# Where the scan's gate products stand: two parts moved from the inverse's last levels to the end of each scan step

## The chip, the cores and the metric

One core of one Trainium2 chip runs the whole program. The metric is the device time of one execution in microseconds. Two kernels are compared by their runs on the same chip.

## The reference, cut to what matters

The model is one inference step through two layers, over 128 context tokens and 512 latent tokens (five blocks of 128). In each layer a mixing part has four branches. The outputs of the branches are weighted by gates and summed:

```
proj  = einsum('blnw,nwd->blnd', branches, w_branch)
gates = sigmoid(h @ w_gate + b_gate)
out   = einsum('blnd,blnd->bld', gates, proj) @ w_out
```

The gates need only `h`, so they can be computed at any time before the projection. One branch is a scan over time in two directions and with four heads, whose state is 64 x 64 per head:

```
sa = einsum('bhvk,bhk->bhv', S, -kk_t)
S  = S * w_t + sa * (kk_t * a_t) + v_t * k_t
y  = einsum('bhvk,bhk->bhv', S, r_t)
```

The rest of a layer (local attention, a convolution, a spatial gate, the mixture of experts) is not touched here.

## The kernel before

**The scan in steps.** The kernel does the scan in chunks of 128 tokens. `STEPS` lists five steps of a layer, numbered 0 to 4 here; a step does one block of the forward and one of the backward direction, so eight (direction, head) pairs side by side. Within a step the recurrence becomes a triangular system. Its inverse `TT` is built on TensorE by doubling: first the 32 x 32 diagonal blocks (four levels, `INNER` = 4, the loop from L1129), then level `INNER` joins them to 64 x 64 (from L1151), and level `INNER + 1` joins those to 128 x 128 (from L1173). Each level has two sets of small products with a copy between them: TensorE makes X (semaphore `x_mm`), ScalarE copies X out of PSUM (L1575, at the last level L1578, semaphore `xm_done`), TensorE multiplies by the other factor (`y_mm`, at the last level `yt_mm`), and VectorE puts the result into the inverse (L1989 and L1991 for the inner levels; L2001, L2006 and L2011 at level `INNER`; L2022 at level `INNER + 1`, semaphore `t_done`). GpSimd copies the four diagonal blocks into `TT` (L819, `tt_done`), which the last level's second products wait for.

**The step's end.** With the inverse there, TensorE makes U from the old state and the values (`u_mm`); then the first two terms of the outputs y (they need nothing new); then, when ScalarE has copied U (L1581, `u_done`), the inverse times U (`sa_mm`). ScalarE negates that into `sa` (L1584, `sa_done`), and TensorE makes the last term of y and the new state (`step_mm`). VectorE adds both up (L2036 to L2043, `step_done`) and goes straight on to the next step's first operations (from L1915), which ScalarE's square root and sigmoids (L1398, L1555, L1556) and TensorE's decay sums wait for.

**The gate products as filler.** The gate product of a layer is cut into 64 units of 320 tokens by 128 columns; each unit has two parts of four k-tiles, and `PARTS` lists these 128 parts in order. Each part is twelve fp32r products of 128 x 128 by 128 x 320. `behind(lo, hi)` issues parts `lo` to `hi` on TensorE. Part 0 of a unit issues eight small products for the modulation ahead of them (`micro_rows`, 128 x 64 rows in the trace), and in odd units two more products (`micro_columns`); its own waits are for the bank (the sigmoid two units back), for the split weights, and for the loaded modulation weights. `behind_out` is ScalarE's side: after part 1 of a unit it copies the modulation row (L1466), takes the sigmoid (L1472) and, in even units, rounds the next 128 x 1024 weight chunk (L1448). `rests_behind` is VectorE's side: the rest of that chunk (L1747), also after part 1 of even units. SyncE's queue loads the modulation weights two units ahead (L669), loads the weight chunks (L663) and stores the gates to HBM (L690), each behind the semaphore of the unit's products or sigmoid.

**Where the parts stand.** The order is written out by hand: each engine's program names the same ranges of parts at the same places. A step owns 13 parts (`STEP_PARTS`). Its first parts fill the waits of the step's preparation; from `part + LEVELS_FROM` on, each of the six levels has one range, `level_parts(part, lev)`, issued between a level's X products and its second products:

```python
    lo = part + LEVELS_FROM + lev
    return lo, closed(part + STEP_PARTS) if lev == LEVELS - 2 else lo + 1
```

So level `INNER` has one part and level `INNER + 1` the rest of the step: `closed` rounds up to a whole unit. In steps 0, 2 and 4 the two levels have parts 0 and 1 of one unit. In steps 1 and 3 level `INNER` has part 1 of a unit, and level `INNER + 1` both parts of the next. That is 12 parts of a layer at these two levels, 24 in all. The rest of a weight chunk (L1747) falls among them in step 1 and step 2 (at level `INNER + 1`) and in step 3 (at level `INNER`).

Of the kernel before, what the change touches and what calls it, by code (L numbers as in the profile page):

```python
# [157 lines left out]
INNER = LEVELS - 3  # L158
# [82 lines left out]
def build(nc, a):  # L241
    ctx = ExitStack()
    with ctx:
# [182 lines left out]
        def bank(b, n=512):  # L426
            return ps[:, b * 512:b * 512 + n]
# [438 lines left out]
        def _(pe):  # L866
# [93 lines left out]
            with pe.Fori(0, DEPTH) as layer:  # L960
# [121 lines left out]
                for s, blocks in enumerate(STEPS):  # L1082
# [72 lines left out]
                            early, late = halves_of(g // 4, h)  # L1155
                            ins = mm(bank(4)[late, g * QB:(g + 1) * QB], gb[early, g, 0, late], Tc[early, g])
                    ins.then_inc(x_mm, 1)
                    behind(*level_parts(part, INNER))
                    pe.wait_ge(xm_done, now.next("xm_done"))
                    pe.wait_ge(ttc_done, now.next("ttc_done", 2))  # L1160
                    pe.sem_inc(waits_settled, 1)
# [15 lines left out]
                        early, late = rows64 if g < 4 else rows64[::-1]  # L1177
                        ins = mm(bank(0)[late, g * HD:(g + 1) * HD], gb[early, g, 0, late], T64[early, g % 4])
                    ins.then_inc(x_mm, 1)
                    behind(*level_parts(part, INNER + 1))  # L1180
                    pe.wait_ge(xm_done, now.next("xm_done"))
                    pe.wait_ge(ttc_done, now.next("ttc_done", 2))
                    pe.wait_ge(tt_done, now.next("tt_done"))
# [20 lines left out]
                    for g in range(8):  # L1204
                        ins = mm(by_row_half(2, g), gk[:, g, 0, :], v_of(g), False, g >= 6)
                    ins.then_inc(u_mm, 1)
                    for g in range(8):
                        of = rows64[g % 2]
                        mm(by_row_half(0, g), ar[of, g // 2, 1, :], S0[of, g // 2], g < 2, False)
# [3 lines left out]
                    for g in range(8):  # L1213
                        ins = mm(bank(2)[:, g * HD:(g + 1) * HD], TT[:, g], ub[:, g])
                    ins.then_inc(sa_mm, 1)
                    pe.wait_ge(sa_done, now.next("sa_done"))
                    for g in range(8):
                        mm(by_row_half(0, g), gb[:, g, 1, :], sa[:, g], False, g >= 6)
# [157 lines left out]
        def _(act):  # L1376
# [111 lines left out]
            with act.Fori(0, DEPTH) as layer:  # L1488
# [62 lines left out]
                for s, blocks in enumerate(STEPS):  # L1551
                    part = SCAN_AT + s * STEP_PARTS
                    root(kss)
                    act.wait_ge(wa_pre, now.next("wa_pre"))
                    A(sw, sw, ACT.Sigmoid)  # L1555
                    A(aa, aa, ACT.Sigmoid).then_inc(wa_done, 1)  # L1556
                    behind_out(closed(part), part + WA_PARTS)
                    act.wait_ge(decay_mm, now.next("decay_mm"))
                    A(rt.rearrange("p d c -> p (d c)"), bank(2), ACT.Exp)
                    A(bt.rearrange("p d c -> p (d c)"), bank(2), ACT.Exp, scale=-1.0)  # L1560
                    A(at_.rearrange("p d c -> p (d c)"), bank(3), ACT.Exp)
                    A(gm.rearrange("p g e -> p (g e)"), bank(4, 8), ACT.Exp).then_inc(exp_done, 1)
                    behind_out(part + WA_PARTS, closed(part + 5))
                    act.wait_ge(tildeT_mm, now.next("tildeT_mm"))
                    nc.scalar.copy(ar[:, :, 0, :], bank(0).rearrange("p (g t) -> p g t", g=4))
                    nc.scalar.copy(bT, bank(2).rearrange("p (g t) -> p g t", g=4)).then_inc(tildeT_act, 1)
                    behind_out(closed(part + 5), closed(part + 6))
                    act.wait_ge(n_mm, now.next("n_mm"))
                    nc.scalar.copy(nb.rearrange("p (g r) t -> p r g t", r=2),
                                   ps[:, 2048:3072].rearrange("p (r c) -> p r c", r=2)[:, :, 0:4 * QB].rearrange("p r (g t) -> p r g t", g=4)  # L1570
                                   ).then_inc(nc_done, 1)
                    behind_out(closed(part + 6), part + LEVELS_FROM)
                    for lev in range(INNER + 1):
                        act.wait_ge(x_mm, now.next("x_mm"))
                        nc.scalar.copy(Xq.rearrange("p g t -> p (g t)"), bank(4, 8 * QB)).then_inc(xm_done, 1)  # L1575
                        behind_out(*level_parts(part, lev))
                    act.wait_ge(x_mm, now.next("x_mm"))
                    nc.scalar.copy(Xc.rearrange("p g t -> p (g t)"), bank(0)).then_inc(xm_done, 1)  # L1578
                    behind_out(*level_parts(part, INNER + 1))
                    act.wait_ge(u_mm, now.next("u_mm"))  # L1580
                    nc.scalar.copy(ub.rearrange("p (g r) v -> p r g v", r=2),  # L1581
                                   ps[:, 1024:2048].rearrange("p (r g v) -> p r g v", r=2, g=8)[:, :, 0:4]).then_inc(u_done, 1)
                    act.wait_ge(sa_mm, now.next("sa_mm"))
                    nc.scalar.mul(sa.rearrange("p g v -> p (g v)"), bank(2), -1.0).then_inc(sa_done, 1)  # L1584
                root(gs2)
                behind_out(closed(NORM_AT), len(PARTS))
                micro_column_out(CHUNKS - 1, 6)
# [108 lines left out]
        def _(dve):  # L1696
# [97 lines left out]
            with dve.Fori(0, DEPTH) as layer:  # L1794
# [111 lines left out]
                for s, blocks in enumerate(STEPS):  # L1906
# [105 lines left out]
                                                  bank(2, 8 * QB)[early, 4 * d * QB:4 * (d + 1) * QB].rearrange("p (g t) -> p g t", g=4),  # L2012
                                                  -1.0, None, ALU.mult)
                    ins.then_inc(ttc_done, 2)
                    rests_behind(*level_parts(part, INNER))
                    dve.wait_ge(tc_done, now.next("tc_done"))
                    dve.wait_ge(ttc_done, now.next("ttc_done", 2))
                    blocks64 = (slice(0, 64), slice(64, P))
# [3 lines left out]
                        ins = V.tensor_scalar(TT[early, 4 * d:4 * d + 4, late], bank(3).rearrange("p (g t) -> p g t", g=8)[early, 4 * d:4 * d + 4],  # L2022
                                              -1.0, None, ALU.mult)
                    ins.then_inc(t_done, 1)
                    rests_behind(*level_parts(part, INNER + 1))

                    dve.wait_ge(step_mm, now.next("step_mm"))
                    for d, blk in enumerate(blocks):
# [23 lines left out]
                    else:  # L2052
                        ins.then_inc(step_done, 1)
                    dve.wait_ge(step_done, now.next("step_done"))

                rests_behind(closed(NORM_AT), len(PARTS))
                y20 = y.rearrange("p b (h c) -> p (b h) c", h=4)
# [368 lines left out]
```

## Time and profile before

| | |
|---|---|
| Median of 3 runs | 2786.13 us (2786.0 to 2787.79) |
| The profiled execution's own time | 2792.74 us |
| Its span, first to last instruction | 2791.2 us |
| Mean granted clock of TensorE in it | 0.885 |
| TensorE products, busy | 2248.3 us (81%) |
| VectorE, busy | 1388.4 us (50%) |
| ScalarE, busy | 995.0 us (36%) |
| GpSimd, busy | 228.9 us (8%) |

The scan of layer 0 lies from about 461 to 829 us of the span, that of layer 1 from about 1830 to 2205 us. Busy shares over the span mix stages with different limits; in the scan the engines work in a chain, and what counts is which of them the next one waits for. The granted clock of TensorE is a share of full speed: 1.00 is 2.4 GHz, 0.50 is 1.2 GHz.

### The profile page before, as it was taken

Reading aid. Unit: us, or ns where it says so; the run is one execution under the profiler, and the core shown is the slowest. Engines: PE = TensorE matmul, PEld = TensorE weight load, DVE = VectorE, ACT = ScalarE, POOL = GpSimd, SP = SyncE. Lnnn points to the kernel's source line nnn. Section 1 sums busy time; section 2 is a strip of 40 time slices with the busy share of each in tenths; the row PEclk is TensorE's granted clock in tenths of the full one; section 3 lists DMA queues with packets and bytes.
Section 4 is the critical chain, followed back from the end, with each engine's and each line's share of the span. In section 5 each row is a group of like instructions: output and inputs, shape, how many; then the busy total and the mean of one; then the engine's idle time right before and its main releaser. Section 6 shows DMA issues by size and latency. Waiting matters only on the chain.

```text
span 2791.2 us, 50199 instructions
## 1 busy us (share of the span) xinstructions
PE 2248.3 (81%) x20372; PEld 1899.2 (68%) x20372; DVE 1388.4 (50%) x1773; ACT 995.0 (36%) x1448; POOL 228.9 (8%) x251
## 2 busy tenths in 40 slices
PE   4998698898888975989459896888888799588980
PEld 2787688787774764777248785877878658467760
DVE  2225834434346544888242275344343373458873
ACT  3113234222220133777241323432232102257771
POOL 0002111101110001000100031111011000200001
PEclk9998899989898977999769998999898799589995
DMA  7114322323226307999722242233233252279986
GB/s 316 61 61 129 99 84 91 104 85 100 92 88 233 141 36 271 396 392 397 282 85 91 86 136 73 74 112 104 88 105 93 104 210 91 113 294 396 398 333 248
DMA packets 102282, 466.89 MB, mean 167 GB/s; under 512 B 12160, under 2 KB 28800, under 8 KB 75008
## 3 DMA queue, kind: packets, MB, share of 16 engines
q1 hardware_dynamic: 81792, 352.36, 34.8%
q0 software_dynamic: 10320, 75.91, 7.3%
q10 hardware_dynamic: 9936, 35.35, 3.1%
q8 instruction: 166, 2.72, 0.4%
q14 instruction: 68, 0.56, 0.1%
HBM read 389.64 MB, written 94.90 MB: 174 GB/s over the span
## 4 chain that ended last, share of the span: by engine, by line
PE 55%; issue 19%; DVE 9%; DMA 6%; ACT 6%; POOL 4%; SPq 0%; DVEq 0%; ACTq 0%; POOLq 0%
PE ps L870 53%; ACT we_hi L1629 3%; PE ps L873 3%; DVE we_lo L2223 2%; POOL wg_lo L763 2%; DMA x_kept<-x 1%; DMA arena<-in_experts 1%; DMA arena<-expert_out,slots 1%; POOL expert_rows L844 1%; DMA expert_out<-rows 1%; DVE arena L2253 1%; DMA rests_last<-hz_lo 1%; DMA arena<-expert_rows 0%; DVE arena L1989 0%; POOL arena L811 0%
## 5 line engine op out<-in xcount | busy, mean ns | idle before, releaser
L2223 DVE TENSOR_TENSOR we_lo<-arena,we_hi 128x2048 fp32r<-128x2048 f32 x150 | 339.3, 2289 | 92.5 <-ACT we_hi L1629 92.5
L870 PE MATMUL ps<-hz_hi,wg_hi 128*128 128x320 f32 x1024 | 349.6, 341 | 24.6 <-DMA rests_last<-hz_lo 19.0
L870 PE MATMUL ps<-arena 32*32 32x32 f32 (+5 forms) x7408 | 295.6, 225 | 53.7 <-DVE arena L1989 14.2
L870 PE MATMUL ps<-hz_hi,wg_lo 128*128 128x320 f32 x1024 | 330.9, 323 | 0.0
L870 PEld LDWEIGHTS ps<-arena 32*32 32x32 f32 (+4 forms) x7408 | 206.8, 120 | 146.7 <-issue 143.7
L1629 ACT CAST we_hi<-arena 128x2048 fp32r<-128x2048 f32 x150 | 282.9, 1912 | 3.2 <-DMA arena<-in_experts 2.9
L873 PE MATMUL ps<-fix,arena 128*128 128x128 f32 x836 | 133.8, 305 | 164.3 <-DMA arena<-expert_rows 65.9
L870 PE MATMUL ps<-rests,wg_hi 128*128 128x320 f32 x768 | 249.8, 325 | 0.0
L873 PEld LDWEIGHTS ps<-fix,arena 128*128 128x128 f32 x836 | 107.8, 156 | 189.1 <-DMA arena<-expert_rows 66.1
L870 PEld LDWEIGHTS ps<-hz_hi,wg_hi 128*128 128x128 f32 x1024 | 204.7, 200 | 39.3 <-issue 22.0
L870 PEld LDWEIGHTS ps<-hz_hi,wg_lo 128*128 128x128 f32 x1024 | 205.9, 201 | 0.0
L870 PE MATMUL ps<-wz_hi,hz_hi 128*128 128x512 f32 (+1 forms) x480 | 181.6, 378 | 17.3 <-DVE x L1723 17.3
L870 PE MATMUL ps<-wz_hi,hz_lo 128*128 128x512 f32 (+1 forms) x480 | 180.7, 376 | 0.0
L870 PE MATMUL ps<-w_lo,hz_hi 128*128 128x512 f32 (+1 forms) x480 | 180.5, 376 | 0.0
L870 PE MATMUL ps<-we_hi,te_hi 128*128 128x512 f32 x400 | 159.4, 399 | 8.8 <-DVE te_lo L2228 8.8
L870 PE MATMUL ps<-we_hi,te_lo 128*128 128x512 f32 x400 | 158.9, 397 | 0.0
L870 PE MATMUL ps<-we_lo,te_hi 128*128 128x512 f32 x400 | 158.7, 397 | 0.0
L870 PEld LDWEIGHTS ps<-rests,wg_hi 128*128 128x128 f32 x768 | 156.3, 204 | 0.0
L763 POOL TENSOR_TENSOR wg_lo<-ring,wg_hi 128x1024 fp32r<-128x1024 f32 x32 | 77.3, 2417 | 769.5 <-ACT wg_hi L1448 769.5
L1840 DVE SCALAR_TENSOR_TENSOR x<-x,cols 128x655 f32<-128x655 f32 x120 | 132.3, 1144 | 2.1
L1739 DVE TENSOR_TENSOR w_lo<-ring,wz_hi 128x2048 fp32r<-128x2048 f32 x24 | 55.0, 2293 | 142.1 <-ACT wz_hi L1423 142.1
L1466 ACT COPY combT<-ps 128x64 f32<-128x64 f32 x128 | 26.8, 210 | 261.3 <-PE ps L870 261.3
(309 smaller groups left out, 4040.0 us busy)
## 6 DMA issues: line engine op xcount, KB each, us to landing
arena<-in_experts SPq DMA_DIRECT2D x150, 1024.0 KB, 8.9
ring<-in_stream SPq DMA_DIRECT2D x26, 2048.0 KB, 8.4
ring<-in_gate_stream SPq DMA_DIRECT2D x64, 512.0 KB, 3.9
arena<-in_mod_stream SPq DMA_DIRECT2D x128, 256.0 KB, 3.1
expert_rows<-in_stream POOLq DMA_DIRECT2D x50, 512.0 KB, 5.6
arena<-expert_rows SPq DMA_DIRECT2D x50, 512.0 KB, 7.1
expert_out<-rows ACTq DMA_DIRECT2D x50, 512.0 KB, 8.2
gates<-arena SPq DMA_DIRECT2D x128, 160.0 KB, 2.6
```

The costliest lines, as they stand in the source:

```text
L763: nc.gpsimd.tensor_tensor(wg_lo[q % 2], wg[q % 2], wg_hi[q % 2].bitcast(F32), ALU.subtract).then_inc(pool_split, 1)
L844: pool.indirect_dma_start(rows_dram, to, hm[:, b, :], None).then_inc(rows_sent, 16)
L870: return nc.tensor.matmul(out, lhsT, rhs, start=start, stop=stop)
L873: return nc.tensor.transpose(out, in_, ident)
L1466: nc.scalar.copy(micro_row[q % 2][:, at:at + MICRO], bank(bk)[:, HALF:HALF + MICRO]).then_inc(mod_rows, 1)
L1629: nc.scalar.copy(we_hi[n % HIS], raw[n % RAW]).then_inc(piece_hi, 1)
L1739: V.tensor_tensor(half_in(w_lo, v), half_in(ring, v), wz_hi[v % 2].bitcast(F32), ALU.subtract).then_inc(wlo_done, 2)
L1840: ins = V.scalar_tensor_tensor(cacc[f], src, cw[:, f, t:t + 1], cacc[f], ALU.mult, ALU.add)
L2223: V.tensor_tensor(we_lo[n % RAW], raw[n % RAW], we_hi[n % HIS].bitcast(F32), ALU.subtract).then_inc(piece_split, 1)
L2253: V.tensor_tensor(te_hid[i % 2], te_silu[i % 2], ps[:, (i % 2) * 512 + FF:(i % 2) * 512 + 2 * FF], ALU.mult).then_inc(hid_done, 1)
```

## The change

In each scan step the parts of level `INNER` are issued behind the U products, ahead of the first two terms of y. Those of level `INNER + 1` are issued behind the product of the inverse and U, ahead of the wait for `sa_done`. ScalarE's side moves with them: the first range behind its copy of U, the second behind its negation into `sa`. VectorE's side moves too: the rest of a chunk at level `INNER` behind the last operation on the inverse (L2022), that of level `INNER + 1` behind the state's update, ahead of the next step's first operation. No part is added or left out, and the order of the parts is the same.

```diff
--- before.py
+++ after.py
@@ -1155,7 +1155,6 @@
                             early, late = halves_of(g // 4, h)
                             ins = mm(bank(4)[late, g * QB:(g + 1) * QB], gb[early, g, 0, late], Tc[early, g])
                     ins.then_inc(x_mm, 1)
-                    behind(*level_parts(part, INNER))
                     pe.wait_ge(xm_done, now.next("xm_done"))
                     pe.wait_ge(ttc_done, now.next("ttc_done", 2))
                     pe.sem_inc(waits_settled, 1)
@@ -1177,7 +1176,6 @@
                         early, late = rows64 if g < 4 else rows64[::-1]
                         ins = mm(bank(0)[late, g * HD:(g + 1) * HD], gb[early, g, 0, late], T64[early, g % 4])
                     ins.then_inc(x_mm, 1)
-                    behind(*level_parts(part, INNER + 1))
                     pe.wait_ge(xm_done, now.next("xm_done"))
                     pe.wait_ge(ttc_done, now.next("ttc_done", 2))
                     pe.wait_ge(tt_done, now.next("tt_done"))
@@ -1204,6 +1202,7 @@
                     for g in range(8):
                         ins = mm(by_row_half(2, g), gk[:, g, 0, :], v_of(g), False, g >= 6)
                     ins.then_inc(u_mm, 1)
+                    behind(*level_parts(part, INNER))
                     for g in range(8):
                         of = rows64[g % 2]
                         mm(by_row_half(0, g), ar[of, g // 2, 1, :], S0[of, g // 2], g < 2, False)
@@ -1213,6 +1212,7 @@
                     for g in range(8):
                         ins = mm(bank(2)[:, g * HD:(g + 1) * HD], TT[:, g], ub[:, g])
                     ins.then_inc(sa_mm, 1)
+                    behind(*level_parts(part, INNER + 1))
                     pe.wait_ge(sa_done, now.next("sa_done"))
                     for g in range(8):
                         mm(by_row_half(0, g), gb[:, g, 1, :], sa[:, g], False, g >= 6)
@@ -1573,15 +1573,17 @@
                     for lev in range(INNER + 1):
                         act.wait_ge(x_mm, now.next("x_mm"))
                         nc.scalar.copy(Xq.rearrange("p g t -> p (g t)"), bank(4, 8 * QB)).then_inc(xm_done, 1)
-                        behind_out(*level_parts(part, lev))
+                        if lev < INNER:
+                            behind_out(*level_parts(part, lev))
                     act.wait_ge(x_mm, now.next("x_mm"))
                     nc.scalar.copy(Xc.rearrange("p g t -> p (g t)"), bank(0)).then_inc(xm_done, 1)
-                    behind_out(*level_parts(part, INNER + 1))
                     act.wait_ge(u_mm, now.next("u_mm"))
                     nc.scalar.copy(ub.rearrange("p (g r) v -> p r g v", r=2),
                                    ps[:, 1024:2048].rearrange("p (r g v) -> p r g v", r=2, g=8)[:, :, 0:4]).then_inc(u_done, 1)
+                    behind_out(*level_parts(part, INNER))
                     act.wait_ge(sa_mm, now.next("sa_mm"))
                     nc.scalar.mul(sa.rearrange("p g v -> p (g v)"), bank(2), -1.0).then_inc(sa_done, 1)
+                    behind_out(*level_parts(part, INNER + 1))
                 root(gs2)
                 behind_out(closed(NORM_AT), len(PARTS))
                 micro_column_out(CHUNKS - 1, 6)
@@ -2012,7 +2014,6 @@
                                                   bank(2, 8 * QB)[early, 4 * d * QB:4 * (d + 1) * QB].rearrange("p (g t) -> p g t", g=4),
                                                   -1.0, None, ALU.mult)
                     ins.then_inc(ttc_done, 2)
-                    rests_behind(*level_parts(part, INNER))
                     dve.wait_ge(tc_done, now.next("tc_done"))
                     dve.wait_ge(ttc_done, now.next("ttc_done", 2))
                     blocks64 = (slice(0, 64), slice(64, P))
@@ -2022,7 +2023,7 @@
                         ins = V.tensor_scalar(TT[early, 4 * d:4 * d + 4, late], bank(3).rearrange("p (g t) -> p g t", g=8)[early, 4 * d:4 * d + 4],
                                               -1.0, None, ALU.mult)
                     ins.then_inc(t_done, 1)
-                    rests_behind(*level_parts(part, INNER + 1))
+                    rests_behind(*level_parts(part, INNER))
 
                     dve.wait_ge(step_mm, now.next("step_mm"))
                     for d, blk in enumerate(blocks):
@@ -2052,6 +2053,7 @@
                     else:
                         ins.then_inc(step_done, 1)
                     dve.wait_ge(step_done, now.next("step_done"))
+                    rests_behind(*level_parts(part, INNER + 1))
 
                 rests_behind(closed(NORM_AT), len(PARTS))
                 y20 = y.rearrange("p b (h c) -> p (b h) c", h=4)
```

## Rows read from the trace of the kernel before

**Rows 1.** The page's first line.

```profile
span 2791.2 us, 50199 instructions
```

**Rows 2.** Step ends, L2022 to L2043, by windows: length, TensorE busy, granted clock, DMA.

```profile
514.28:529.46 15.18, 13.53 (x142) 0.89 0.17 46
587.81:609.75 21.94, 20.29 (x136) 0.56 0.03 9
...
814.38:828.67 14.29, 10.87 (x128) 1.00 0.04 14
...
sum 186.18, PE 166.15; mean PE 16.61
```

**Rows 3.** The timeline of step 2 in layer 0, its last two levels and end.

```profile
657.20 0.48 PE L870 MATMUL ps<-arena,x 32*32 32x32 f32 x32 [0.61 <-DVE arena L1989]
657.61 0.43 PE L870 MATMUL ps<-arena,silu_c_padded 128*32 128x64 f32 x16
657.63 1.47 DVE L2001 COPY arena<-arena 32x128 f32<-32x128 f32 x4
657.77 1.70 POOL L819 COPY arena<-arena 32x256 f32<-32x256 f32 x4 [21.88 <-DVE arena L1991]
...
659.92 0.71 PE L870 MATMUL ps<-arena 32*32 32x32 f32 x48
660.67 0.59 DVE L2006 TENSOR_SCALAR arena<-ps 32x128 f32<-32x128 f32 x2 [1.57 <-PE ps L870]
...
661.41 0.68 PE L870 MATMUL ps<-arena,x 64*64 64x64 f32 x16 [0.78 <-DVE arena L2006]
662.02 0.41 PE L870 MATMUL ps<-hz_hi,wg_hi 128*128 128x320 f32 x1
662.13 0.59 ACT L1578 COPY arena<-ps 128x512 f32<-128x512 f32 x1 [4.02 <-PE ps L870]
...
663.97 0.68 PE L870 MATMUL ps<-arena 64*64 64x64 f32 x16
664.80 0.86 DVE L2022 TENSOR_SCALAR arena<-ps 64x256 f32<-64x256 f32 x2 [2.32 <-PE ps L870]
665.76 1.11 PE L870 MATMUL ps<-scan_state_scaled,arena 64*128 64x64 f32 x16 [1.11 <-issue]
...
668.84 0.58 ACT L1581 COPY x<-ps 128x512 f32<-128x512 f32 x1 [3.15 <-PE ps L870]
...
673.59 0.60 ACT L1584 ACTIVATE x<-ps 128x512 f32<-128x512 f32 x1 [4.17 <-PE ps L870]
...
674.24 0.99 PE L870 MATMUL ps<-x 128*128 128x64 f32 x7 [0.69 <-ACT x L1584]
```

**Rows 4.** VectorE groups by line: busy, mean ns | idle before them, releaser.

```profile
L2006 DVE TENSOR_SCALAR arena<-ps 32x128 f32<-32x128 f32 x20 | 5.7, 286 | 9.9 <-PE ps L870 9.8
L2022 DVE TENSOR_SCALAR arena<-ps 64x256 f32<-64x256 f32 x20 | 8.4, 422 | 30.0 <-PE ps L870 29.8
```

**Rows 5.** Windows with TensorE's clock: step 2's inner levels; y in steps 2, 3.

```profile
641.45:645.20 3.75, 1.18 (x66) 1.00 0.16 52
645.20:648.05 2.85, 2.18 (x82) 0.51 0.00 0
648.05:651.55 3.50, 3.50 (x16) 0.50 0.27 80
652.03:655.60 3.57, 2.87 (x123) 1.00 0.02 5
668.73:671.60 2.87, 2.87 (x33) 1.00 0.00 0
742.78:748.15 5.37, 5.37 (x34) 0.50 0.01 3
```

**Rows 6.** VectorE's rest of a weight chunk, in the groups by line.

```profile
L1747 DVE TENSOR_TENSOR wg_lo<-ring,wg_hi 128x1024 fp32r<-128x1024 f32 x32 | 39.4, 1230 | 22.1 <-ACT wg_hi L1448 21.0 <-issue 0.3
```

**Rows 7.** The timeline of TensorE at the decay sums of step 3.

```profile
685.08 1.13 PE L870 MATMUL ps<-arena,scan_sums 128*128 128x256 f32 x4 [0.78 <-ACT arena L1556]
```

## The prediction

> **What bounds the kernel now.** I start from the profiled execution: a span of 2791.2 us [rows 1], 2792.74 us by its own time, 6.6 us above the median of the runs shown. The change touches only the ten scan steps (five in each of two layers), so I read the scan. I cut out the ten step ends, from VectorE's last operation on the inverse (L2022) to the new state (L2043), with TensorE's granted clock beside each [rows 2]. The reader should see that the same work takes 14.29 us at clock 1.00 (one step end of the ten), 15.2 to 15.4 us at 0.89 (four) and 21.9 to 22.6 us at 0.55 to 0.57 (five). TensorE is busy nearly all that time, so the slow ends don't wait more: they run at 1.2 instead of 2.4 GHz. All ten last 186.18 us; at full clock they would last 142.9, so the clock costs 43.3 us there.
>
> Then I read one step in order of time [rows 3]. TensorE, ScalarE and VectorE hand on to each other, and a gate part between them costs path time where it is longer than the wait that it fills.
>
> **Level INNER.** In step 2 the X products start at 657.20; modulation rows and the part fill TensorE from 657.61 until the second products start at 659.92, so 2.31 us stand there. Twelve gate products alone take 1.95 us (662.02 to 663.97 at the next level), so the modulation rows take 0.36. Without them the second products wait for ScalarE's copy of X. Its double-sized sibling L1578 takes 0.59 us, so they end by about 659.06. But L2006, which they feed, stands behind four copies on VectorE (L2001) that end at 659.10; these become the limit. L2006 then starts right behind L2001, and what is saved is exactly VectorE's idle time before L2006: 9.9 us over ten steps [rows 4] (1.57 in step 2). Behind the U products the same part covers nothing: the next work, the first two y terms, needs no one, and they hide ScalarE's copy of U (0.58 us) already. So it costs its whole length there. Per layer that is five parts of 1.95, three sets of modulation rows of 0.36 and two pairs of column products. I have no row for a pair: between 0 and 0.36 us, taken as 0.30, nearer the modulation rows because it too loads 128-column weights. This makes 11.4 us a layer and 22.9 for both. Net: 22.9 - 9.9 = **+13.0 us**.
>
> **Level INNER + 1.** Step 2: products start at 661.41, the part at 662.02, the second products at 663.97. ScalarE's copy ends at 662.72; GpSimd's diagonal blocks are there at 659.47. So these products could start at about 662.75, which leaves 1.1 of the 2.32 us of VectorE's idle time before L2022. Over ten steps that idle time is 30.0 us [rows 4], and in step 3 of both layers a chunk rest of 1.23 us lies in the same gap and hides 2.5 more. Saved: 30.0 + 2.5 - 11.0 = 21.5 us. At the new place the parts fill the wait for `sa`, 0.69 us in each step [rows 3], and the rest is on the path. Per layer there are seven parts, two sets of modulation rows and one column pair, 14.7 us; for both layers 29.3. Net: 29.3 - 6.9 - 21.5 = **+0.9 us**.
>
> **The queues the moved work passes.** ScalarE's sigmoid, row copy and chunk rounding now stand between U and `sa`. They start when the part ends, and the y terms (2.87 us [rows 5]) and the product with the inverse lie ahead of `sa`: nothing. Those of the last range run beside the state's products. SyncE's loads and gate stores go out later by the same few us, as do their users: nothing, and if a buffer ran late a part would wait for it. GpSimd's copies, done at 659.47 in step 2, have 1.7 us to spare: the second products would start at about 661.2 there, L2006 being 1.57 us earlier (663.97 - 1.22 - 1.57). VectorE's chunk rests are different. At level INNER (step 3) the rest runs beside U. At level INNER + 1 (steps 1 and 2) it now stands at the head of the next step's chain, whose end TensorE awaits: in step 3 the decay sums start after 0.78 us of idleness, released by ScalarE's sigmoid [rows 7], which follows VectorE. I take the whole 1.23 us [rows 6], four times: **+4.9 us**; the lower bound is 0, if the chain had slack.
>
> **The clock.** This is the large term, and it has two signs. Full clock at all step ends would give back the 43.3 us. But the level work loses its fill. See what such a stretch does in step 2's inner levels [rows 5]: from 641.45 to 648.05 TensorE ran small products with waits between, the clock was 1.00 until 645.20 and 0.50 from there. The part that followed ran at 0.50, 3.50 us instead of 1.95, and at 652.03 the clock was back. After the change every step has a stretch of that kind: in step 2 from the last inner part (its end is the edge of the window that ends at 655.60 [rows 5]) to U (665.76 - 1.57 - 1.22 = 662.97), 7.4 us against the 6.6 us of the example. Before, the gap without a part ahead of U was 663.97 to 665.76, and even behind that the clock was down for most of five of the ten ends. So I expect the clock to fall ahead of U in all ten steps. Dense products of the end don't bring it back: the y terms take 5.37 us at 0.50 in step 3 against 2.87 in step 2, busy throughout [rows 5]. The moved part of level INNER does, as in the example. The loss per step: U has as many products as the y terms, 2.5 us; the 64 x 64 products about 0.3 (from 0 to their doubling, 1.2; taken near the bottom because waits dominate there); and the part and the start of y until the clock returns, from 0 to 1.75 (the 1.55 of a whole part and some 0.2 of y). The example, where it returned only behind the part, says the upper half: 1.2. Together 4.0 us a step (2.5 to 5.4), **+40 us** for ten. From there on the end holds full clock: y ran through at 1.00 in step 2, and the gap ahead of the new state that now stops TensorE is filled. So **-43.3 us** on the other side. The median, 6.6 us below the profiled execution, may have had one slow end less (8.3 us); then it is -35.
>
> **Sum.** 13.0 + 0.9 + 4.9 + 40 - 43.3 = +15.5 us. On the median of 2786.13 us that is 2801.6; in a profiled execution about 2808.
>
> **Rivals.**
>
> First, **the clock follows how busy TensorE is**, so it is back as soon as U runs without a gap, and holds to the end of the step; the 40 us vanish. The Trainium skill, "TensorE: Matmul & The Clock Gate", section "What's actually happening", says that the gate is set by how busy the array has been recently; by that rule this rival would be the outcome. For it: the new ends have no gap behind the wait for `t_done`, as U, the parts, y and the state stand one behind the other. Against it: y at 0.50 was busy 5.37 of 5.37 us [rows 5], so busy time alone doesn't raise the clock here. It decides at one place, U of each step: if U takes 3 us there, and not 5.4, the time is 2786.1 + 18.8 - 43.3 = 2761.6, **faster**. Chance 0.15.
>
> Second, **the clock returns early and the chunk rests are hidden**: the loss is 3.0 us a step and VectorE's chain has slack. 13.9 + 30 - 43.3 = +0.6, or +5.5 with the rests: 2787 to 2791.6, no change that can be told. The place is the start of the moved part; it decides if less than 0.5 us of it runs at 0.50. Chance 0.14.
>
> Third, **one part isn't enough to raise the clock**, and each end stays at 0.50 as five do now. Per step, U 2.5, the part 1.55, y 2.5, the product with the inverse 1.7 (1.99 us from 671.60, the edge of a window [rows 5], to 673.59 [rows 3], by y's ratio of 1.87), the last parts about 2 and the state about 2.5 (by the same ratio): 12.7 us, ten times 127 - 43.3 + 18.8 = +102, 2889. Against it is the example, where one part sufficed. Chance 0.03.
>
> That the change doesn't do what it says has no room: no semaphore is added, and each moved range waits for things older than before.
>
> **How the numbers follow.** The forecast, slower, has 0.68. A measurement of this kernel can tell about 0.2%, 5.6 us, from no change. Slower by more: the forecast and the third rival, 0.71; within: 0.14; faster: the first, 0.15. The forecast's own bounds: with 3.2 us lost per step and the rests hidden, +2.6; with 5.0 and one slow end fewer before, +33.8. The range of 2783 to 2820 takes both in and leaves out the first and third rivals, 0.18.
>
> **What would show it.** Right: in each of ten steps the clock goes to 0.50 between the last inner part and U, U takes 5 to 5.5 us, the clock is 1.00 from y to the state, and the stretch from L2022 to L2043 lasts about 23 us in steps 0, 2 and 4 and 24 in steps 1 and 3, with the parts in it. L2006 follows L2001 without a gap, idle time before L2022 is 1.1 us, and the decay sums of steps 2 and 3 start 1.2 us later behind L2043. Wrong: U at 3 us (first rival), a moved part that is at full clock from its start (second), or a state product at 0.50 (third).

## The result, and the profile after

| | before | after |
|---|---|---|
| Median, same chip | 2786.74 us (2786.0 to 2787.79, 4 runs) | 2834.4 us (2814.75 to 2837.61, 4 runs) |
| Ratio, 95% interval | | 1.0156 (1.0109 to 1.0203) |
| Profiled execution, its span | 2792.74 us, 2791.2 us | 2837.61 us, 2836.0 us |
| Mean granted clock in it | 0.885 | 0.868 |

The change makes the kernel slower by 47.7 us. The forecast was slower, by 15.5 us, with a range that ended 34 us above the kernel before: the direction held, the size did not.

First the ten step ends, from VectorE's first operation on the last level's result (L2023 now) to the new state (L2044 now). They are the windows of [rows 2] in the changed kernel, with length, TensorE's busy time, granted clock, DMA share and GB/s:

```profile
513.45:536.20 22.75, 21.79 (x198) 0.74 0.15 43
594.95:618.00 23.05, 22.10 (x207) 0.80 0.17 50
673.34:694.62 21.28, 20.32 (x195) 0.79 0.07 22
...
sum 226.16, PE 213.03; mean PE 21.30
```

Before, the ends were of two kinds, five near 15 and five near 22 us. Now all ten take 21.2 to 23.9 us at 0.74 to 0.82. The timeline of step 2, beside [rows 3], says where in an end the clock is low:

```profile
667.70 1.47 DVE L2003 COPY arena<-arena 32x128 f32<-32x128 f32 x4
...
669.37 0.59 DVE L2008 TENSOR_SCALAR arena<-ps 32x128 f32<-32x128 f32 x2 [0.20 <-PE ps L870]
...
670.10 1.12 PE L870 MATMUL ps<-arena,x 64*64 64x64 f32 x16 [0.78 <-DVE arena L2008]
671.26 0.59 ACT L1579 COPY arena<-ps 128x512 f32<-128x512 f32 x1 [3.05 <-PE ps L870]
...
672.08 1.12 PE L870 MATMUL ps<-arena 64*64 64x64 f32 x16 [0.86 <-ACT arena L1579]
673.34 0.86 DVE L2023 TENSOR_SCALAR arena<-ps 64x256 f32<-64x256 f32 x2 [2.16 <-PE ps L870]
674.30 1.97 PE L870 MATMUL ps<-scan_state_scaled,arena 64*128 64x64 f32 x16 [1.10 <-issue]
676.20 3.67 PE L870 MATMUL ps<-arena,x 128*128 128x64 f32 x16
...
683.27 1.11 PE L870 MATMUL ps<-scan_state_scaled,arena 64*128 64x64 f32 x16
```

U is the pair of rows from 674.30. Its first sixteen products take 1.97 us, and the same sixteen of y behind the moved part take 1.11 at 683.27. The 64 x 64 products take 1.12 instead of the 0.68 of [rows 3]. L2008 follows L2003 by 0.20 us where 1.57 lay between them. Windows of the same step show the clock itself:

```profile
666.00:674.30 8.30, 4.28 (x177) 0.67 0.51 148
674.30:680.40 6.10, 6.10 (x49) 0.50 0.01 3
680.40:682.41 2.01, 2.01 (x11) 0.50 0.30 89
682.41:694.62 12.21, 12.21 (x141) 1.00 0.07 22
```

U and the modulation rows of the moved part are busy throughout and stay at 0.50; so do the first seven of the part's own twelve products; from 682.41 to the end of the step the clock is 1.00. This is the picture that the prediction drew, and all ten steps show it. VectorE's groups, beside [rows 4]:

```profile
L2023 DVE TENSOR_SCALAR arena<-ps 64x256 f32<-64x256 f32 x20 | 8.4, 422 | 20.5 <-PE ps L870 20.4
L2008 DVE TENSOR_SCALAR arena<-ps 32x128 f32<-32x128 f32 x20 | 5.7, 286 | 1.5 <-PE ps L870 1.3
```

The idle time before L2008 is gone, as forecast (9.9 us, now 1.5). That before L2023 fell from 30.0 to 20.5 and not to 11.

To see the rest I cut the scan into seven stretches and summed each over its steps, in the two profiled executions: A from the new state to the next second sigmoid (L1556; eight gaps), B to VectorE's copy at L1970 (L1968 before), C to L2008 (L2006), D to L2023 (L2022), E to ScalarE's copy of U, F to `sa`, G to the new state.

| us | A | B | C | D | E to G | ten steps | all else |
|---|---|---|---|---|---|---|---|
| before | 35.6 | 127.6 | 338.4 | 50.4 | 186.2 | 738.2 | 2053.0 |
| after | 40.8 | 145.6 | 330.0 | 38.4 | 226.2 | 781.0 | 2055.0 |
| difference | +5.2 | +18.1 | -8.5 | -12.0 | +40.0 | +42.8 | +2.1 |
| forecast | +4.9 | 0 | -9.9 | -18.5 | +39.0 | +15.5 | 0 |

The forecast of E to G is 22.9 + 29.3 - 6.9 for the parts, 25 for U and 12 for the part at low clock, less 43.3. Stretch B, which the prediction did not look at, holds most of what is missing. Two lines of its windows, step 1 of layer 0 and the sum, in the changed kernel:

```profile
541.01:560.42 19.41, 17.59 (x114) 0.74 0.25 80
...
sum 145.64, PE 137.93; mean PE 13.79
```

and in the kernel before:

```profile
534.28:549.00 14.72, 12.95 (x114) 1.00 0.33 105
...
sum 127.57, PE 120.44; mean PE 12.04
```

It is the same work, 114 products, at a lower clock. Why it fell there is seen at the decay sums with which B begins. Here is the timeline at them, before, in steps 1 and 2:

```profile
534.94 1.99 PE L870 MATMUL ps<-arena,scan_sums 128*128 128x256 f32 x8 [1.42 <-ACT arena L1556]
...
614.74 1.99 PE L870 MATMUL ps<-arena,scan_sums 128*128 128x256 f32 x8 [0.17 <-ACT arena L1556]
```

and after:

```profile
541.68 2.99 PE L870 MATMUL ps<-arena,scan_sums 128*128 128x256 f32 x8 [2.24 <-ACT arena L1556]
...
624.29 3.67 PE L870 MATMUL ps<-arena,scan_sums 128*128 128x256 f32 x8 [4.49 <-ACT arena L1556]
```

TensorE now stands idle for 2.24 and 4.49 us ahead of them, and the clock falls while they run. Over the eight step starts that follow a step of the same layer, this idle time was 10.8 us and is 25.7; at 1.00 in all eight before, the clock falls in five of them now.

### The profile page after: what moved, and what is told of

It reads as the page before. It is cut to its first block, busy times and chain, and to the rows that moved or that the text cites. A ratio compares the mean times of both kernels' runs of the same rounds, so it can differ in the third digit from the quotient of the medians.

```text
span 2836.0 us, 50199 instructions
## 1 busy us (share of the span) xinstructions
PE 2259.6 (80%) x20372; PEld 1912.2 (67%) x20372; DVE 1389.1 (49%) x1773; ACT 995.8 (35%) x1448; POOL 228.7 (8%) x251
## 4 chain that ended last, share of the span: by engine, by line
PE 55%; issue 19%; DVE 9%; DMA 7%; ACT 6%; POOL 4%; SPq 0%; DVEq 0%; ACTq 0%; POOLq 0%
PE ps L870 52%; ACT we_hi L1631 3%; PE ps L873 3%; DMA arena<-in_experts 2%; POOL wg_lo L763 2%; DVE we_lo L2225 2%; DMA x_kept<-x 1%; DMA arena<-expert_out,slots 1%; POOL expert_rows L844 1%; DMA expert_out<-rows 1%; DMA rests_last<-hz_lo 1%; DVE arena L2255 1%; DMA arena<-expert_rows 0%; DVE arena L1991 0%; POOL arena L811 0%
## 5 line engine op out<-in xcount | busy, mean ns | idle before, releaser
L870 PE MATMUL ps<-hz_hi,wg_hi 128*128 128x320 f32 x1024 | 357.4, 349 | 24.7 <-DMA rests_last<-hz_lo 19.0
L870 PE MATMUL ps<-arena 32*32 32x32 f32 (+5 forms) x7408 | 303.2, 228 | 70.9 <-DVE arena L1991 14.3
L870 PE MATMUL ps<-hz_hi,wg_lo 128*128 128x320 f32 x1024 | 337.3, 329 | 0.0
L870 PEld LDWEIGHTS ps<-arena 32*32 32x32 f32 (+4 forms) x7408 | 213.4, 123 | 162.3 <-issue 158.6
L870 PEld LDWEIGHTS ps<-hz_hi,wg_hi 128*128 128x128 f32 x1024 | 211.0, 206 | 39.1 <-issue 22.5
L870 PEld LDWEIGHTS ps<-hz_hi,wg_lo 128*128 128x128 f32 x1024 | 212.5, 207 | 0.0
```

Source lines behind the costliest of these rows:

```text
L870: return nc.tensor.matmul(out, lhsT, rhs, start=start, stop=stop)
```

## The experiments

Each run has its own kernel before on the same chip. The stages outside the scan, which no kernel here changes, took 2034 to 2057 us between the profiled executions, so where 20 us matter I compare the ten steps in the traces, and give the ratio of the runs beside it. The traces are one execution of each kernel. In the expectations below the second to fifth experiments are rests_early, after_warm, before_warm and after_warm_start, and "the third of these" is ahead_of_u.

| kernel | ratio, 95% interval | ten steps | A | B | C | D | E | F | G |
|---|---|---|---|---|---|---|---|---|---|
| before | | 738.2 | 35.6 | 127.6 | 338.4 | 50.4 | 46.2 | 68.4 | 71.6 |
| after | 1.0156 (1.0109 to 1.0203) | 781.0 | 40.8 | 145.6 | 330.0 | 38.4 | 65.7 | 86.6 | 73.8 |
| after_again | 1.0137 (1.0076 to 1.0199) | 780.7 | 40.8 | 146.8 | 327.8 | 39.4 | 65.7 | 86.3 | 73.9 |
| inner_back | 1.0224 (1.0184 to 1.0264) | 801.5 | 40.8 | 142.3 | 337.7 | 33.3 | 64.6 | 89.2 | 93.6 |
| before_warm | 0.9904 (0.9872 to 0.9936) | 704.2 | 35.6 | 135.2 | 339.8 | 50.4 | 40.3 | 47.5 | 55.4 |
| after_warm | 0.9987 (0.9961 to 1.0012) | 739.1 | 40.8 | 148.7 | 332.1 | 33.4 | 40.9 | 69.4 | 73.9 |
| rests_only | 1.0058 (1.0031 to 1.0086) | 757.3 | 40.8 | 134.7 | 340.3 | 50.4 | 44.4 | 72.5 | 74.1 |
| rests_early | 1.0145 (1.0093 to 1.0197) | 781.7 | 35.6 | 135.8 | 328.6 | 39.0 | 65.7 | 98.2 | 78.7 |
| start_warm_only | 1.0082 (1.0053 to 1.0112) | 774.8 | 40.8 | 135.9 | 333.1 | 39.8 | 65.7 | 85.7 | 73.9 |
| after_warm_start | 0.9861 (0.9795 to 0.9928) | 713.3 | 40.8 | 139.0 | 316.4 | 32.7 | 41.3 | 69.4 | 73.9 |
| before_warm_start | 0.9889 (0.9823 to 0.9954) | 707.2 | 35.6 | 133.9 | 340.3 | 54.2 | 40.3 | 47.5 | 55.4 |
| after_warm_rests | 0.9876 (0.9829 to 0.9923) | 702.3 | 35.6 | 134.4 | 314.0 | 33.2 | 40.9 | 69.3 | 74.7 |
| ahead_of_u | 0.9908 (0.9874 to 0.9942) | 718.2 | 35.6 | 136.3 | 337.2 | 33.0 | 64.2 | 47.5 | 64.4 |
| ahead_of_u_warm | 0.9892 (0.9864 to 0.9921) | 714.9 | 35.6 | 134.0 | 341.0 | 32.8 | 68.5 | 47.5 | 55.4 |

**after_again**, the changed kernel a second time.

> The changed kernel, nothing altered, for a second profiled execution. Which of the terms recur? Theory: the fall ahead of U is set by where the parts stand: in all ten steps 6.57 us from the first result of the last level to ScalarE's copy of U, the state's products at 1.00 in nearly all; and the falls in the step starts are a consequence of the change too, so the stretch from the second sigmoid to the copy at L1970 sums to 140 to 150 again (127.6 in the kernel before), the ten steps to 775 to 787. Rival: the falls in the starts were this one execution's; then that stretch sums to 127 to 134 and the ten steps to 760 to 770. Stages outside the scan, which the change does not touch, may differ by 20 us either way.

E, F and B came out at 65.7, 86.3 and 146.8, within 1.2 us of the first execution: both the fall ahead of U and the slower step starts came back, though not in the same starts.

**inner_back**: level `INNER` undone (all three engines), the last level's parts left behind the inverse's product. TensorE's side of the edit, against the changed kernel:

```diff
                     ins.then_inc(x_mm, 1)
+                    behind(*level_parts(part, INNER))
...
                     ins.then_inc(u_mm, 1)
-                    behind(*level_parts(part, INNER))
```

> The change with level INNER's range put back to its old place on all three engines; only the last level's parts stand behind the product with the inverse. Theory (the clock falls where the parts are missing ahead of U, and only parts bring it back): the stretch without a part now runs from the last level's X products to the end of the product with the inverse, so the clock is at 0.50 over U, the y terms and that product in most steps (about 6.7 us each), and at 1.00 in the state's products. In the sum +0.9 for the last level, +4.9 for the chunk rests, -43 and about +54: some 2800 us, clearly above the kernel before. Rival (the part behind U is what costs, by its length, and the clock follows TensorE's busy time): 2750 to 2792 us, U at 3 us.

It became slower than the changed kernel (2841.5 us, where some 2800 were expected). The windows from ScalarE's copy of U to `sa` (y's first terms and the product with the inverse), two of ten and the sum:

```profile
516.51:525.43 8.92, 8.92 (x49) 0.50 0.00 0
...
846.50:855.42 8.92, 8.92 (x49) 0.50 0.01 2
...
sum 89.18, PE 89.18; mean PE 8.92
```

TensorE is busy for 8.92 of 8.92 us, in all ten steps, and stays at 0.50. So without a part ahead of y the clock does not come back before the last level's parts, and in one step not behind them either: G grows to 93.6 us. The part behind U is paid for on the path and earns more than it costs.

**before_warm** and **after_warm**: products whose result nobody reads (128 x 128 by 128 x 320, fp32r, into a bank that is free) in TensorE's waits. In before_warm they take no path time: its ends last 14.3 us, as the one end at full clock does in [rows 2].

```diff
+            def warm(issued, count):
+                i = units(closed(issued))
+                pe.wait_ge(sig_done, now.value("sig_done", 2 * (i - 1)))
+                for _ in range(count):
+                    mm(bank(6 + i % 2, HALF), hz_hi[:, 0, 0:P], hz_hi[:, 0, 0:HALF])
...
                     ins.then_inc(yt_mm, 1)
+                    warm(closed(part + STEP_PARTS), 6)
...
                     ins.then_inc(sa_mm, 1)
+                    warm(closed(part + STEP_PARTS), 4)
```

That is before_warm. after_warm has six behind `yt_mm` too, and four in each of the four waits of the last two levels.

> The kernel before, with thrown-away products of 128 x 128 by 128 x 320 added in two waits of each step's end: six in the wait for t_done ahead of U, four in the wait for sa. Theory: the clock no longer falls in the ends, all ten last about 14.3 us, and the time is 43 us lower, about 2744 us. Rival (the clock in the ends falls for another reason, or the products of the end can't hold it): 2780 us or more, with 21.9 us ends still there.

> The change, with products added that are thrown away: four of 128 x 128 by 128 x 320 in each wait of the last two levels (four waits) and six in the wait for t_done, written to the bank of the next gate unit ahead of its first product. They compute nothing that is used. Theory (the clock is what makes the change slow): the clock stays at 1.00 from the last inner part to the state in all ten steps, U takes 3 us again, and the time is 40 us or more below the change, about 2790 us or less; what is left over the full-clock sum are the falls in step starts. Rival (the parts' length on the path and the new waits cost it, the clock is a side effect): within 10 us of the change, or slower by what the added products take (2 us a step).

The windows of the ends in before_warm, the same cut as [rows 2]:

```profile
588.21:602.50 14.29, 14.21 (x165) 1.00 0.04 13
...
sum 143.25, PE 138.84; mean PE 13.88
```

All ten are at 1.00. The ends gave back 186.18 - 143.25 = 42.9 us, as the prediction said (43.3); but B grew by 7.6 us, and the ten steps are shorter by 34.0 (median 2757.5 us, expected about 2744). Why B grew is seen at step 2's decay sums, where 0.17 us of idle time stood before:

```profile
607.50 3.68 PE L870 MATMUL ps<-arena,scan_sums 128*128 128x256 f32 x8 [3.08 <-ACT arena L1565]
```

The windows of the ends in after_warm, step 2 and the sum:

```profile
661.59:679.18 17.59, 17.57 (x201) 1.00 0.08 27
...
sum 184.12, PE 180.37; mean PE 18.04
```

They take 184.1 us instead of 226.2, all but one at 1.00 (step 0 of layer 1: 0.96). D to G together are 47.0 us shorter than in the changed kernel, B and C 5.2 longer, the ten steps 41.9 shorter. B stays high, at 148.7.

**rests_only** and **rests_early**: VectorE's chunk rest of the last level alone moved as in the change, and alone moved back.

```diff
-                    rests_behind(*level_parts(part, INNER + 1))
                     dve.wait_ge(step_mm, now.next("step_mm"))
...
                     dve.wait_ge(step_done, now.next("step_done"))
+                    rests_behind(*level_parts(part, INNER + 1))
```

> The kernel before with one part of the change alone: VectorE's chunk rest of the last level moved from behind the inverse to behind the state's update (four of the ten steps); all gate parts stay where they were. Measured by the ten steps' sum from the second sigmoid to the new state plus the stretch from the state to the next sigmoid, since stages outside the scan vary between executions. Theory: the rest stands alone on the chain, 4 times 1.23 = +4.9 us from the state to the next sigmoid (35.6 becomes 40.5 to 40.8) and nothing else; the stretch from the sigmoid to the copy at L1968 stays near 127.6, because TensorE arrives late at its wait where the end before ran at 0.50; the ten steps 738.2 become 741 to 746 and the median is 3 to 8 us above the kernel before. Rival: the delay alone makes the clock fall in the starts of steps 2 and 3 of both layers, as it seemed in the changed kernel; then the stretch behind the sigmoid grows by 1.5 to 4 us in each of the four, to 134 to 143, and the ten steps take 749 to 758.

> The change, but VectorE's chunk rest of the last level stands ahead of its wait for the state's products instead of behind the state's update. Theory (the rest costs its own 1.23 us in four step starts, the clock falls there because TensorE now comes earlier to its wait): 4 to 8 us less than the change, the starts of steps 2 and 3 (state to sigmoid) back from 5.6 to 4.3 us. Rival (the delay by the rest is what lets the clock fall in the step starts): the clock at 1.00 in the starts of steps 2 and 3 too, 12 us less or more. If the rest was hidden after all: the same time as the change.

With the rest alone moved the ten steps take 19.1 us more, and the kernel 0.6%. 5.2 us are the rest itself (A). B takes 7.1 more, by the rival's way, though in layer 0 only: 4.5 in step 2 and 1.7 in step 3, but also 1.7 in step 1, ahead of which no rest stands. Step 2's decay sums in rests_only:

```profile
614.94 3.78 PE L870 MATMUL ps<-arena,scan_sums 128*128 128x256 f32 x8 [4.10 <-ACT arena L1556]
```

and that step's B: 16.75 us at 0.69, where the kernel before takes 12.28 at 0.98. The wait grew by 3.9 us, of which the rest's delay is 1.3; in this execution TensorE was also done sooner behind the state. The remaining 6.8 us are in C to G, mostly one more end at 0.50. In rests_early A and B give back 5.2 and 9.9 us. The clock is at 1.00 in all four starts that the rest had delayed, as the rival said, and falls in three others. But F and G take 11.6 and 4.9 more; F's windows, three of the ten:

```profile
835.77:849.10 13.33, 13.33 (x79) 0.50 0.07 21
1907.48:1920.81 13.33, 13.33 (x79) 0.50 0.07 21
...
2143.84:2156.07 12.23, 12.23 (x62) 0.50 0.04 13
```

In these three steps one part did not bring the clock back: the third rival, in three of ten. The ten steps together took what the changed kernel takes, so the lower median of these runs cannot be put down to the rest.

**start_warm_only, after_warm_start, before_warm_start, after_warm_rests**: six thrown-away products ahead of the decay sums, in the changed kernel, in after_warm and in before_warm; the last is after_warm_start with the rest early as well.

```diff
                     behind(closed(part), part + WA_PARTS)
+                    warm(part + WA_PARTS, 6)
```

> The change with six thrown-away products in each step's wait ahead of the decay sums and none elsewhere. Theory (about 18 of the unforeseen microseconds are falls of the clock in the step starts, on their own): the stretch from the second sigmoid to the transposed operands sums to about 128 to 135 us instead of 145.7, the ends stay as slow as in the change, and the time falls by 10 to 18 us, to some 2816 to 2824. Rival (the starts slow down only through what the ends leave behind): no gain, 2830 us or more.

> The change with the thrown-away products of the third experiment and six more in each step's wait ahead of the decay sums. In the third experiment the stretch from the second sigmoid to the transposed operands still summed to 148.7 us over ten steps, against 127.6 us in the kernel before. Theory (the clock falls there as well, since TensorE reaches the wait for the sigmoids earlier): the sum goes back to about 128 us and the time falls by some 20 us, to about 2758. Rival (the stretch is longer because of the chunk rest or a late weight chunk): the sum stays near 148 and the time near 2779.

> The kernel before with the thrown-away products of the fourth experiment and six more in the wait ahead of the decay sums. Theory: its starts, 135.2 us in the fourth experiment, go back to about 128, so 5 to 8 us less: about 2750. The difference to the run beside it is then what the change costs at full clock: 18.8 us by the prediction's sum, so some 2750 against 2769 or less. Rival (the added products delay the decay sums): no gain, 2757 or more.

> The change with the thrown-away products in the levels' waits and in the starts (as in the fifth experiment), and the last level's chunk rest ahead of VectorE's wait for the state's products (as in the second). Theory: the two gains add, the step starts lose another 5 us of waiting and little else is left, so 5 to 10 us below the fifth: about 2748, below both kernels. Rival (TensorE's wait is what the thrown-away products fill, and with it shorter they come onto the path): the same as the fifth, 2756 or more.

The six fill 0.9 us of the idle time in each start (step 1: 2.25 becomes 1.37). B goes from 145.6 to 135.9 in the first and from 148.7 to 139.0 in the second: 9.7 us, half of what it had grown by. The rest of the gain of 17 us in the median of start_warm_only lies outside the scan (its ten steps are shorter by 6.2 us), so that hit is partly luck. So is that of after_warm_start (2756.2 us, expected about 2758): of the 25.8 us by which its ten steps are shorter than those of after_warm, C gave 15.7. In before_warm there was nothing to gain: before_warm_start took 2763.9 us, not 2750, and was not faster than after_warm_start on the same chip, where 18.8 us had been expected. after_warm_rests does best in the ten steps, 702.3 us:

```profile
463.28:810.58 347.30, 313.62 (x5857) 0.97 0.32 102
1814.04:2169.01 354.97, 316.41 (x5864) 0.97 0.31 100
sum 702.27, PE 630.03; mean PE 315.02
```

Its median, 2754.5 us, lies between the theory (2748) and the rival (2756); its interval lies within that of before_warm_start and overlaps that of before_warm, which throws away far less.

**ahead_of_u, ahead_of_u_warm**: the kernel before with one line moved, the last level's parts behind its second products, ahead of the wait for `t_done`; the second with the thrown-away products at the step's start and behind the inverse's product.

```diff
                     ins.then_inc(x_mm, 1)
-                    behind(*level_parts(part, INNER + 1))
...
                     ins.then_inc(yt_mm, 1)
+                    behind(*level_parts(part, INNER + 1))
```

> The kernel before with one line moved on TensorE: the last level's parts stand behind its second products, ahead of the wait for t_done, so that they fill that wait and stand right ahead of U. Nothing is thrown away. Theory: the parts give back ScalarE's wait (-21.5 us) and cost their length less the 1.1 us wait (+18.3), so about -3 at full clock, and as they stand right ahead of U the clock is at 1.00 from U to the product with the inverse in all ten steps; some state products may still run at 0.50. Together 25 to 30 us less than before, about 2757. Rival (the stretch from the first part to these lets the clock fall, as it did when they stood behind the product with the inverse): 2780 us or more.

> The third of these with thrown-away products in two places, four in the wait for sa and six ahead of the decay sums. Theory: clock at 1.00 in all ends and starts, some 8 us below the third, at about 2748, the best of all. Rival (TensorE's wait for sa is too short to matter): the same as the third.

Both beat the two kernels of this study, the first with no product added (2767.5 us, 23 less than the kernel before beside it; expected were 25 to 30). D falls from 50.4 to 33.0 us, since nothing stands between the last level's products, and F is at full clock in all ten. E pays for the parts (46.2 becomes 64.2), and in five of the ten steps the clock was down for a part of E (0.71 to 0.88). What remains is the wait for `sa`, behind which the clock fell in seven of the ten ends; here are one in which it fell and one in which it did not:

```profile
747.27:754.66 7.39, 6.74 (x56) 0.59 0.00 0
...
2107.11:2112.62 5.51, 4.86 (x75) 1.00 0.00 0
```

In ahead_of_u_warm G is at 55.4 as expected, but E and C are 8.1 us longer, and the 2748 us that I expected did not come (2764.9).

## Why the prediction was right in sign and wrong in size

**The path, right in sum.** after_warm against before_warm shows the change with the clock at 1.00 from D to G, but for a part of one step. F and G grow by 21.9 and 18.5 us (forecast 22.9 and 29.3 - 6.9 = 22.4), A by 5.2 (4.9); C falls by 7.7 (9.9) and D by 17.0 (21.5); E is 0.6 longer. That is +21.4 against +18.8. The closeness is partly luck: G is 3.9 us below the forecast, 0.3 to 0.6 in each step, and the saving in D is 4.5 short, as VectorE's idle time ahead of its first operation on the last level's result is 15.4 us there, where I had left 11.0. C moves with the clock of the inner levels as well, so its share is uncertain: after_warm_start lies only 6.1 us above before_warm_start in the ten steps, because its C is 23.9 lower. The pair of column products, put at 0.30 us without a row, takes 0.21 to 0.31 us at full clock in the trace of the kernel before; the reason given for it does not hold, as the modulation rows load 32 columns there and not 128.

**The clock ahead of U, right in place and low in size.** It fell in all ten steps, twice over, and in all ten of inner_back. after against after_warm: E +24.8 (forecast 25), F +17.2 (12), D +5.0 (3), together 47.0 instead of 40. The part stayed at 0.50 longer than the 1.2 us a step that I chose, near the upper bound of 1.75 that the prediction had worked out; I took a value between the bounds where the only row at hand, the part of [rows 5], spoke for the bound.

**The clock given back at the ends, right.** -42.9 in before_warm against -43.3, and the state's products at 1.00 in all ten ends of the changed kernel.

**The starts, not in the sum.** The step that failed is the one on the queues that the moved work passes: "I take the whole 1.23 us, four times: +4.9 us". The rest does cost that, 5.2 us. But the row that I read for it, the decay sums of [rows 7] with 0.78 us of idleness ahead of them, shows TensorE waiting. I asked only when it would start, not what a longer wait does to the clock behind it, and the clock term counted the step ends alone. The starts (B) took 18.1 us more.

Two things lengthen that wait. The rest delays its end, by 1.3 us in four starts. And the ends at full clock, the very gain that I had counted, bring TensorE to it sooner: what it still has to do behind the state of step 1 takes 4.82 us at a mean clock of 0.51 before, and 1.92 us at 1.00 in before_warm, where the idle time in the eight starts grows from 10.8 to 20.1 us and B by 7.6. How the 18.1 us divide between the two is not shown. rests_only has 7.1 and before_warm 7.6, 14.7 together, but not all of the 7.1 is the rest's doing; taken the other way, from the changed kernel, moving the rest back gave 9.9, 5.5 of it in the four starts that the rest had delayed.

After the change the idle time is 25.7 us. Where it is longest the clock falls most often: in none of the eight starts before (10.8 us), in four of before_warm (20.1), and in five, six, five and seven of after, after_again, inner_back and after_warm, which all have 25.7. It is not all that decides: rests_early, with 21.4, has three, and which start it is differs between executions.

Added up: 2.6 on the path, 7.0 ahead of U, 0.4 at the ends, 18.1 in the starts and -0.8 in C make 27.3 us, and 15.5 + 27.3 are the 42.8 us of the ten steps. The other 2.1 us of the profiled executions lie outside the scan, and the medians differ by a few us more.

**The rivals.** The first, a clock that is back as soon as U runs without a gap, fell at the place that was named for it: U's products take 5.6 us in step 2, near the 5.4 that spoke against this rival and far from its 3, and E is 6.57 us in each step where it is 4.03 at full clock. The rule of the Trainium skill behind it ("TensorE: Matmul & The Clock Gate", section "What's actually happening"), that the gate follows how busy the array has been, is not borne out by busy time as the profile counts it: inner_back's windows are busy 8.92 of 8.92 us at 0.50. The second fell at the start of the moved part, 2.01 us of which ran at 0.50 in step 2 (its limit was 0.5), and the rests are not hidden (A). The third, one part that does not raise the clock, was given 0.03 for all ten steps; it happened in three steps of rests_early, and in none of the twenty of after and after_again.

**Open.** The six products at the start brought back only half of B; what else lets the clock fall there was not found, and why a fall comes in one execution and not in the next at the same idle time neither. C came down to 316.4 and 314.0 us in the two kernels with thrown-away products at the levels and at the start. Its mean clock is 0.96 and 0.97 there, against 0.91 with those at the levels alone (after_warm, 332.1 us) and 0.91 with those at the start alone (start_warm_only, 333.1), so neither does it by itself; why both do was not found. Thrown-away products in every wait of the scan were not tried.

## What to carry to other kernels

Filler on TensorE can be worth more than the wait it fills: here its place set the clock of the products behind it (47.0 us in D to G, after against after_warm), so ask of each stretch it leaves what the clock will do there, and of each place it comes to whether dense work follows. When a stage gets faster, look at the next wait of the same engine: here TensorE's idle time ahead of the decay sums grew from 10.8 to 20.1 us, and the starts took back 7.6 of the 42.9 us that the ends had given. Put filler that must be on the path right ahead of the dense products (ahead_of_u, one line moved: 0.9% faster than the kernel before).

## What was not expected of the hardware

Work that is thrown away pays. Ten products a step in two waits made the kernel before faster by 1.0% (before_warm), and 28 a step turned a change that costs 1.6% into one that is 1.4% faster than the kernel before (after_warm_start).

TensorE can be busy without a gap for many microseconds and stay at half clock: 13.33 of 13.33 us in rests_early, with a whole gate part among them, where the same part raised the clock in seven other steps of that execution.

Stages that none of these kernels touch differ by up to 23 us between profiled executions, half of what this change costs. A sum over the changed stage told apart what medians of four to six runs did not: start_warm_only is 16.8 us below the changed kernel by its median and 6.2 by the ten steps.
